# Seven block products for the up projections of layer 0, all their weight sums on GpSimd, modulation blocks spread over both layers

## The reference

```python
def swiglu(h, w1, w3, w2):
    return (jax.nn.silu(h @ w1) * (h @ w3)) @ w2

def first_block(x, c, positions, ada_w, ada_b, ...):
    cos, sin = rope_tables(positions)
    cond = jax.nn.silu(c)
    for l in range(DEPTH):
        mod = cond @ ada_w[l] + ada_b[l]
        sh1, sc1, g1, sh2, sc2, g2, sh3, sc3, g3 = jnp.split(mod, N_MOD, axis=-1)
        h = modulate(x, norm_ffn1[l], sh1, sc1)
        x = x + 0.5 * (1.0 + g1)[:, None] * swiglu(h, ffn1_w1[l], ffn1_w3[l], ffn1_w2[l])
        h = modulate(x, norm_mix[l], sh2, sc2)
        y = token_mix(h, cos, sin, ...)
        x = x + (1.0 + g2)[:, None] * y
        h = modulate(x, norm_ffn2[l], sh3, sc3)
        x = x + 0.5 * (1.0 + g3)[:, None] * swiglu(h, ffn2_w1[l], ffn2_w3[l], ffn2_w2[l])
    return x
```

## Time and profile before

| | us |
|---|---|
| median of 3 runs | 2769.98 (2768.59 to 2771.56) |
| profiled execution | 2770.82 |
| its span, first to last instruction | 2769.0 |
| PE busy | 2710.7 (98% of the span) |
| PE weight loads | 2443.6 (88%) |
| VectorE (DVE) busy | 1493.8 (54%) |
| ScalarE (ACT) busy | 494.7 (18%) |
| GpSimd (POOL) busy | 109.6 (4%) |

### The profile page before, as it was taken

One profiled execution on the slowest core, in us unless ns is written; L12 is line 12 of the kernel. 1 busy time (PEld: TensorE's weight loads), 2 busy tenths in 40 slices (PEclk: granted clock), 3 DMA queues, 4 the chain that ended last, 5 costly groups with the idle time before them and its releaser, 6 DMA issues.

```text
span 2769.0 us, 38584 instructions
## 1 busy us (share of the span) xinstructions
PE 2710.7 (98%) x16024; PEld 2443.6 (88%) x16024; DVE 1493.8 (54%) x3086; ACT 494.7 (18%) x867; POOL 109.6 (4%) x98
## 2 busy tenths in 40 slices
PE   7999999999999999999999999999999999999998
PEld 6899888888889999888878899988888998888888
DVE  4586764553447666465463466535335652323565
ACT  1011343420100100243232100003110011111000
POOL 0000000000000340000000141000000000000000
PEclk9999999999999999999999999999999999999999
DMA  9886621325887444441132444442334444333442
GB/s 365 308 326 261 241 94 62 122 93 181 287 303 268 155 170 171 161 152 62 62 123 106 167 168 168 153 167 107 137 108 152 160 160 152 130 137 116 153 157 92
DMA packets 74718, 460.76 MB, mean 166 GB/s; under 512 B 8340, under 2 KB 9248, under 8 KB 28208
## 3 DMA queue, kind: packets, MB, share of 16 engines
q1 hardware_dynamic: 73408, 451.44, 44.8%
q0 software_dynamic: 1136, 6.86, 0.7%
HBM read 457.17 MB, written 1.09 MB: 165 GB/s over the span
## 4 chain that ended last, share of the span: by engine, by line
PE 92%; DVE 3%; DMA 2%; DVEq 1%; ACT 1%; issue 0%; ACTq 0%
PE psum L518 20%; PE psum L564 16%; PE psum L710 14%; PE psum L650 9%; PE psum L880 8%; PE psum L762 4%; PE psum L954 3%; DMA aring<-astream 2%; PE psum L586 2%; PE psum L665 2%; PE psum L900 2%; PE psum L827 2%; PE psum L774 1%; PE psum L540 1%; PE psum L853 1%; DVE aring L1781 1%
## 5 line engine op out<-in xcount | busy, mean ns | idle before, releaser
L518 PE MATMUL psum<-h,ring 128*128 128x256 f32 x1648 | 358.6, 379 | 1.4 <-DVE arena L1752 0.8
L518 PEld LDWEIGHTS psum<-h,ring 128*128 128x128 f32 x1648 | 312.7, 190 | 45.4 <-DVE arena L1752 1.1
L564 PE MATMUL psum<-aring,ring 128*128 128x256 f32 x1408 | 304.7, 379 | 1.7 <-issue 1.7
L564 PEld LDWEIGHTS psum<-aring,ring 128*128 128x128 f32 x1408 | 267.4, 190 | 38.7 <-issue 2.4
L710 PE MATMUL psum<-arena 128*128 128x128 f32 x2112 | 251.3, 276 | 2.2 <-DVE arena L1656 2.2
L710 PEld LDWEIGHTS psum<-arena 128*128 128x128 f32 x2112 | 244.2, 193 | 2.4 <-DVE arena L1656 2.4
L880 PE MATMUL psum<-h,ring 128*128 128x256 f32 x1024 | 236.6, 384 | 0.0
L880 PEld LDWEIGHTS psum<-h,ring 128*128 128x128 f32 x1024 | 193.3, 193 | 26.5 <-issue 1.9
L710 PE MATMUL psum<-arena,ring 128*128 128x128 f32 x1584 | 191.8, 275 | 0.2 <-DVE arena L1643 0.2
L710 PEld LDWEIGHTS psum<-arena,ring 128*128 128x128 f32 x1584 | 184.5, 192 | 0.6 <-issue 0.3
L518 PE MATMUL psum<-arena,ring 128*128 128x256 f32 x720 | 157.7, 380 | 6.0 <-DVE arena L2387 3.1
(11 more groups left out here) (423 smaller groups left out, 3650.7 us busy)
## 6 DMA issues: line engine op xcount, KB each, us to landing
ring<-wstream SPq DMA_DIRECT2D x351, 1024.0 KB, 4.8
aring<-astream SPq DMA_DIRECT2D x128, 512.0 KB, 5.3
arena<-astream SPq DMA_DIRECT2D x16, 512.0 KB, 18.0
arena<-wstream SPq DMA_DIRECT2D x3, 1024.0 KB, 20.6
arena<-decays POOLq DMA_DIRECT2D x2, 1024.0 KB, 7.8
sq<-decays POOLq DMA_DIRECT2D x2, 1024.0 KB, 5.4
kst<-const SPq DMA_DIRECT2D x1, 1280.5 KB, 7.7
x<-xT SPq DMA_DIRECT2D x1, 1024.0 KB, 4.9
```

Of the source, the lines that this page charges most:

```text
L518: mm = pe.matmul(out, lhsT=tile_at(at[0] % RING, t), rhs=rhs(k), start=k == 0, stop=k == kt - 1)
L564: mm = pe.matmul(psum[:, s % 4, n * T:(n + 1) * T], lhsT=tile_at(slot, n * KD + k), rhs=rhs(k), start=k == 0, stop=k == KD - 1)
```

## The change

- Layer 0's first up stage does slabs 8 to 21 with seven products, its second one slabs 2 to 21: 34 slabs more. The host lays their weights out for it. Early slabs 0 to 7 stay plain.
- GpSimd makes all four weight sums in all four stages, with a drain ahead of the third and of the fourth; VectorE's `second_weight_sums` is gone. In the three stages after the first one, the sums of slabs 2 and 3 may begin when the stage before is used up.
- Modulation blocks are due at other turns: nine right behind the first 16, ahead of the first hidden tile; then 15 over slabs 8 to 18; 28 in place of 44 beside layer 0's second up stage; 24 over slabs 2 to 19 of layer 1's first up stage and 10 in the down stage behind it. SyncE issues the first ones ahead of slab 8.
- `gains` and `modulation` are computed later; angles use other buffers (`ms`, `std`, positions in `sinT`); `memT` is loaded after the last up stage of layer 1; `up_tokens` lies elsewhere.

```diff
@@ def ada_turns():
-    turn |= {16 + n: EARLY + n // 3 for n in range(42)}
-    turn |= {58 + n: 22 + n * 11 // 14 for n in range(14)}
-    turn |= {72 + n: 33 + n // 2 for n in range(12)}
-    turn |= {84 + n: SLABS_1 - 36 + n // 2 for n in range(6)}
-    turn |= {90 + n: SLABS_1 - 33 + n // 2 for n in range(44)}
-    turn |= {134 + n: SLABS_1 - 11 + n for n in range(10)}
+    turn |= {16 + n: EARLY - RING + n // 3 for n in range(9)}
+    turn |= {25 + n: EARLY + n * 11 // 15 for n in range(15)}
+    turn |= {40 + n: 22 + n * 11 // 14 for n in range(14)}
+    turn |= {54 + n: 33 + n // 2 for n in range(12)}
+    turn |= {66 + n: SLABS_1 - 36 + n // 2 for n in range(6)}
+    turn |= {72 + n: SLABS_1 - 33 + n * 20 // 28 for n in range(28)}
+    turn |= {100 + n: SLABS_1 - 11 + n for n in range(10)}
+    turn |= {110 + n: SLABS_1 + 2 + n * 18 // 24 for n in range(24)}
+    turn |= {134 + n: SLABS_1 + 22 + n for n in range(10)}
...
-        quick_up = [SLABS_1, 2 * SLABS_1 - 33]
+        quick_up = [0, SLABS_1 - 33, SLABS_1, 2 * SLABS_1 - 33]
+        quick_begin = [EARLY, 2, 2, 2]
...
@@ SyncE
-                if i == EARLY + 2:
+                if i == EARLY:
                     for a in range(HEAD, HEAD + AHEAD):
                         sp.dma_start(aring[:, a % AHEAD], astream[a]).then_inc(ada_landed[a % AHEAD], 16)
-                while i >= EARLY + 3 and b < DEPTH * ADA and TURN[b - AHEAD] + RING <= i:
+                while b < DEPTH * ADA and TURN[b - AHEAD] + RING <= i:
...
@@ GpSimd
-            def weight_sums(first, s):
-
+            def weight_sums(rounds, s):
+
+                first = quick_up[rounds]
                 i = first + s
...
-                pool.wait_ge(slab_used, max(i - 1, first))
+                if s >= quick_begin[rounds] + 2:
+                    pool.wait_ge(slab_used, i - 1)
+                elif rounds == 0:
+                    pool.wait_ge(ada_used, HEAD)
+                else:
+                    pool.wait_ge(slab_used, first)
                 nc.gpsimd.tensor_tensor(new[:, 0], w[:, 2], w[:, 3], ALU.add)
-                nc.gpsimd.tensor_tensor(new[:, 1], w[:, 0], w[:, 2], ALU.subtract).then_inc(first_sums, 1)
+                nc.gpsimd.tensor_tensor(new[:, 1], w[:, 0], w[:, 2], ALU.subtract)
+                pool.drain()
+                nc.gpsimd.tensor_tensor(new[:, 2], new[:, 0], w[:, 0], ALU.subtract).then_inc(up_summed, 1)
+                pool.drain()
+                nc.gpsimd.tensor_tensor(new[:, 3], w[:, 1], new[:, 2], ALU.subtract).then_inc(up_summed, 1)
...
-            pool.wait_ge(arena_free, 1)
+            pool.wait_ge(slab_used, quick_up[3] + NF)
             pool.dma_start(memx, memT).then_inc(mem_in, 16)
...
@@ PE, early_pairs
                     slab_wait(at[0])
-                    pe.wait_ge(bank_free, s - EARLY + 1 if s < EARLY + 4 else s - 3)
-                    for n in range(2):
-                        for k in range(KD):
-                            mm = pe.matmul(psum[:, s % 4, n * T:(n + 1) * T], lhsT=tile_at(at[0] % RING, n * KD + k),
-                                           rhs=h[:, k], start=k == 0, stop=k == KD - 1)
-                    mm.then_inc(slab_used, 1)
-                    at[0] += 1
+                    pe.wait_ge(bank_free, max(2 * (s - EARLY) + 2 if s < EARLY + 4 else 0, s - 3))
+                    seven_products(0, s, lambda k: h[:, k])
...
-                if layer == 0:
-                    pairs(lambda k: h[:, k], "operands_of_act", first=bare)
-                else:
-                    quick_pairs(lambda k: h[:, k], "operands_of_act")
+                quick_pairs(lambda k: h[:, k], "operands_of_act")
...
@@ VectorE
+            def quad_swiglu(s, turn, first):
+
+                dve.wait_ge(slab_used, cnt.next("slab_used"))
+                c, b = 4 + 4 * (s % 2), 2 * (s % 4)
+                pb = psum[:, b + 1].rearrange("p (a t) -> p a t", a=4)
+                D()
+                add_products(c, psum[:, b], pb[:, 0:2], pb[:, 1:3], lambda: None).then_inc(inputs_for_act, 1)
+                TT(quads[:, c + 2], quads[:, 2], psum[:, b, 3 * P:], ALU.subtract).then_inc(bank_free, 1)
+                ada_sums(turn)
+                D()
+                dve.wait_ge(functions_for_dve, cnt.next("functions_for_dve"))
+                TT(hidden[:, s].rearrange("p (a t) -> p a t", a=2), quads[:, c:c + 2], quads[:, c + 2:c + 4],
+                   ALU.mult)
+                before_down(s, first)
+                D()
...
             def early_swiglu():
 
-                for s in range(NF):
+                dve.wait_ge(functions_for_dve, cnt.next("functions_for_dve"))
+                token_sums(h, up_tokens, 0, 4).then_inc(tokens_ready, 1)
+                ada_sums(EARLY - 1)
+                for s in range(EARLY):
...
+                for s in range(EARLY, NF):
+                    quad_swiglu(s, s, NF)
                     if s == NF - 5:
                         angles()
```

More of the change, by code:

```diff
@@ L545, in first_slab, with pairs @@
                 at[0] += 1
-            def pairs(rhs, event, after=None, first=None):
-                if first is not None:
-                    first_slab(first, lambda n, k: n * KD + k)
+            def pairs(rhs, event, after=None):
                 cnt.seen[event] += KD
-                begin = 0 if first is None else 1
-                for s in range(begin, NF):
+                for s in range(NF):
                     slot = at[0] % RING
@@ L571, in pairs, with seven_products @@
                 cnt.seen["bank_free"] += NF
+            def seven_products(rounds, s, rhs):
+                slot = at[0] % RING
+                new = up_sums[:, s % 2]
+                for name, (bk, c) in up_banks.items():
+                    if name == "M6":
+                        if s == quick_begin[rounds]:
+                            pe.wait_ge(tokens_ready, rounds + 1)
+                        pe.wait_ge(up_summed, up_sums_before(rounds, s) + 1)
+                    if name == "M3":
+                        pe.wait_ge(up_summed, up_sums_before(rounds, s) + 2)
+                    out = psum[:, 2 * (s % 4) + bk, c * P:(c + 1) * P]
+                    for m in range(4):
+                        x1, x2, t = rhs(2 * m), rhs(2 * m + 1), up_tokens[:, m]
+                        w, v = dict(M1=(tile_at(slot, m), x1[:, 0:P]),
+                                    M2=(tile_at(slot, 4 + m), x2[:, 0:P]),
+                                    M3=(new[:, 3, m], x2[:, P:T]),
+                                    M4=(tile_at(slot, 12 + m), t[:, 3]),
+                                    M5=(new[:, 0, m], t[:, 0]),
+                                    M6=(new[:, 2, m], t[:, 1]),
+                                    M7=(new[:, 1, m], t[:, 2]))[name]
+                        mm = pe.matmul(out, lhsT=w, rhs=v, start=m == 0 and name in ("M1", "M5"),
+                                       stop=m == 3, skip_group_check=True)
+                mm.then_inc(slab_used, 1)
+                at[0] += 1
             def early_pairs():
@@ L1268, in first_gate @@
                 E(gate4[:, 0], gate4[:, 0], ACT.Silu, bias=col(FIRST, 0)).then_inc(functions_for_dve, 1)
-            def swiglu_gate():
-                first_gate()
-                for s in range(1, NF):
-                    act.wait_ge(slab_used, cnt.next("slab_used"))
-                    E(gate4[:, s % 4], psum[:, s % 4, 0:T], ACT.Silu).then_inc(functions_for_dve, 1)
-                cnt.seen["slab_used"] += 11
             def quick_swiglu_gate():
@@ L1284, in quick_swiglu_gate @@
                 for s in range(2, NF):
-                    act.wait_ge(inputs_for_act, cnt.next("inputs_for_act"))
-                    gate = quads[:, 4 + 4 * (s % 2):6 + 4 * (s % 2)]
-                    E(gate, gate, ACT.Silu).then_inc(functions_for_dve, 1)
+                    quad_gate(s)
                 cnt.seen["slab_used"] += NF - 2 + 11
@@ L1727, in down @@
+                ada_sums(turn)
+                cnt.next("slab_used")
+                dve.wait_ge(functions_for_dve, cnt.next("functions_for_dve"))
+                TT(hidden[:, 1], gate4[:, 2], psum[:, 2, T:2 * T], ALU.mult).then_inc(bank_free, 1)
+                ada_sums(turn + 1)
+                for s in range(2, NF):
+                    quad_swiglu(s, turn + s, turn + NF)
             def down(gcol, turn=None, scaled_to=None, gain=None):
@@ L2113, in mixer_inputs @@
                 ada_sums(base + 38)
+                gains(layer, 1)
+                modulation(layer, 2)
                 dve.wait_ge(functions_for_dve, cnt.next("functions_for_dve"))
@@ L2369, in _ @@
                 modulation(layer, 1)
-                gains(layer, 1)
                 down(24, turn=base + 22, **unscaled(bare, 1))
@@ L2377, in _ @@
                 ada_sums(base + 33)
-                modulation(layer, 2)
-                gains(layer, 2)
                 mixer_inputs(layer)
```

138 lines of the change are left out of this document (41 added, 97 removed).

## The result

The changed kernel takes 2805.45 us (median, 2803.64 to 2807.58) against 2769.28 us for the kernel before (2767.31 to 2771.56) on the same chip: ratio 1.0131, interval 1.0113 to 1.0148, so 36.2 us slower. I had forecast 14.2 us slower, 2784 us.

A forecast was written before the change was run, and what follows sets the result against it. PE was taken as the bound, busy 2710.7 of 2769.0 us. Saving -22.2, GpSimd late +6.2, down stages +17, norms +9.8 and clock +3.4 gave +14.2 on 2770.0: 2784 us, range 2756 to 2808.

The forecast's parts named there:

- The lock: VectorE instructions with two SBUF inputs and GpSimd's SBUF-reading sums exclude each other, the loser waiting; VectorE loses up to 1.1 us each time.
- the three steps that follow from it: PE waits on late GpSimd in up stages, +6.2 us; on late VectorE at down stages, +17; at norms, +9.8.
- step 2: Down stages: VectorE falls behind in the up stages and frees banks late, so PE waits; +17 us, ends 8 and 18.
- the three tails: PE's waits for late VectorE where three down stages begin: 8, 6.4 and 5 us, less 2.2 us of today's wait.
- what costs nothing: First stage's start and moved small work: early ada blocks, token sums and slab 8's load fall in idle time; 0 us.
- Rival (d): First stage's start is not covered, ada blocks or slab 8 late: adds 3 to 8 us to any case; no chance given.
- the clock: After PE waits of over 2 us the granted clock falls: six at 0.85 us, less today's 1.7; +3.4 us, ends -1.7 and 8.5.
- step 1: Two up stages with ada blocks: GpSimd's sums fall behind and PE waits 4.9 and 1.3 us; +6.2 us, ends 0 and 20.
- (a): Up stages: no lasting contention, sums slip between VectorE's operations; -22.2 us, 2748 us, chance 0.15.
- (b): The lock at light ends: 8 us for tails, 6 for norms, nothing for pace and clock; -8, 2762 us, chance 0.2.
- (c): GpSimd as the bound: drains near 0.5 us make 7.6 us a slab; +34, 2804 us, chance 0.15.
- the 2770 to 2800 us that I held likeliest: Whole kernel: the lock as priced, forecast 2784 us, chance 0.5.

## Why the prediction was right in its direction and wrong in its size

**The mechanism held.** The lock was the cause: the run with one-input blocks gave back 26 of the 36 us, and the three steps that follow from it came to 8.5, 17.9 and 8.4 us where 6.2, 17 and 9.8 were forecast. The signs named ahead are there: PE waits on GpSimd in the two stages with blocks, on VectorE at three down stages, on h at three norms, and 17 ada blocks take 2.28 us. The price of 0.99 us for a sum behind an ada block, carried on in a line from shorter operations, came out too (2.25 us against 1.27, L465 at 150.63). The drain on GpSimd, which no row had shown, costs 0.15 us as assumed (66.56 - 65.15 - 1.26):

```profile
65.15 1.26 POOL L465 TENSOR_TENSOR arena<-ring 128x512 f32<-128x512 f32 x1
66.56 1.27 POOL L467 TENSOR_TENSOR arena<-arena,ring 128x512 f32<-128x512 f32 x1
```

Within step 2 the shares differ: the three tails are 10.6, 5.5 and 2.9 us and not 8, 6.4 and 5. The first was forecast too small because the angles lasted 13.6 us instead of 7.6: their operations with a single SBUF input were blocked too (L2339 below, against 0.29 us once GpSimd was done). The prediction names this case from the Trainium skill ("SBUF — State Buffer", "Who interferes with whom"), some 5 us for the dozen tensor_scalars, and leaves it out of the sum. The trace sides with the page: had I taken it, the first tail would have been over by 2 us instead of under by 3.

```profile
164.30 1.20 DVE L2339 TENSOR_SCALAR std<-std 128x256 f32<-128x256 f32 x1
...
171.00 0.29 DVE L2339 TENSOR_SCALAR std<-std 128x256 f32<-128x256 f32 x1
```

**The step that failed: "what costs nothing".** "slab 8 ... is wanted at 74.6: covered by 10 us" looked at slab 8's own load, and that was indeed in time. What was not covered was VectorE's path to the banks. I had listed the early ada blocks and token sums as work for an idle stretch, without following (a) what stands ahead of blocks 22 to 24 in SyncE's queue, 1.8 MB of constants, and (b) what PE asks for at slab 8, five tiles by the `s - 3` in the diff where I took two. Rival (d) named the failure and its size, "3 to 8 us", but not that it was the likely case. It took 8.0 us and one fall of the clock. Runs with either of its causes taken out gave back 5.2 and 7.5 us, and started the first down stage 4.9 and 4.7 us earlier.

**The term that was mis-sized: the clock.** I took six waits at 0.85 us, the middle between "no fall" and 1.7, for want of a row that said how often a wait brings one. The run with four waits of 4.5 us says always, that with 2.2 us once in four, that with 1.1 us never; in the changed kernel it fell in all seven places, behind waits of 2.0 (with 0.7 just after it) to 10.6 us. At 1.7 each less today's that is 10.2 us, and with 1.9, 2.7 and 2.8 behind the three longest, 12.4. I had priced 3.4, so 9 us are missing here, 8 at the start and 2.3 in step 1. Even so the upper end for this term, 8.5 us, was too low.

**Rivals.** (a) and (b) are out by the tails; (c) came near in time (2804) by luck, as it is not what happened: drains cost 0.15 us and not 0.5, and GpSimd's own lateness 8.5 us, not 20. The result lies above the 2770 to 2800 us that I held likeliest, though the mechanism is that case's.

## What to carry to other kernels

Before moving work to GpSimd, list what VectorE does meanwhile with two SBUF inputs (and the copies, casts and tensor_scalars with one), and count both directions of the blocking; then look for another place for the VectorE operations, not for the GpSimd ones. Follow each "hidden" step to the semaphore value that the waiting engine asks for, and to everything queued ahead of its DMA. In these traces a standstill of TensorE of some 3 us or more costs itself and 1.4 to 3.4 us of clock, and one near 2 us is a toss.

## What the runs showed of the hardware

- GpSimd's add of 128x512 f32 takes 1.27 us alone, 1.43 to 1.52 in the mean over the changed kernel, and up to 2.32 where an ada block began just ahead of it (L464 at 829.08).
- A tensor_scalar of VectorE with one SBUF input, 0.29 us alone, takes 1.20 beside a GpSimd sum, and so does a cast of that size (L2327 at 160.32); a tensor_reduce of 128x1024 stays at 1.21 us.
- Equal waits of 2.2 us on TensorE, 16 us apart, brought a fall of the clock once and none three times; those of 1.1 us never, those of 4.5 us each time.
- The cost of a fall does not go by the length of the wait. It was 1.7 us behind four waits of 4.5 to 4.7 us, but some 3 us behind others of 2.7 us (the norm above) and 4.6 us (the third tail of the run with later loads, 0.56 over 7 us), and 2.7 and 2.8 us behind 10.6 and 5.5 us. What decides between them isn't settled.
